# RWKV inputs: the receptance and the output gate's blended input computed for the 512 latent tokens alone

## What is computed

```python
def rwkv_prepare(h, mu, w_rkv, ...):
    xx = centred_shift(h) - h
    xr, xw, xk, xv, xa, xg = h[None] + xx[None] * mu[:, None, None, :]
    r, k, v = jnp.einsum('sbtd,sde->sbte', jnp.stack([xr, xk, xv]), w_rkv)
    ...                                   # decay from xw, a from xa
    g = jax.nn.sigmoid(xg @ g1) @ g2
    ...
    yc_f, yc_b, st_f, st_b = bidir(cxt, s0, s0, need_ctx)     # need_ctx is False in this layer
    yl_f, yl_b, _, _ = bidir(lat, st_f, st_b, True)
    out_l = readout(lat, yl_f, yl_b)
```

## Time and profile before

| quantity | value |
|---|---|
| median of three runs | 3681.42 us (3680.19 to 3684.13) |
| span of the profiled execution | 3676.6 us |
| its mean granted TensorE clock | 0.963 of full speed |
| TensorE busy | 3407.3 us (93%) |
| VectorE busy | 1631.8 us (44%) |
| ScalarE busy | 1158.3 us (32%) |
| GpSimd busy | 400.1 us (11%) |
| share of TensorE in the chain that ended last | 82% |

### The profile page before, as it was taken

One profiled execution on the slowest core, in us unless ns is written; L12 is line 12 of the kernel. 1 busy time (PEld: TensorE's weight loads), 2 busy tenths in 40 slices (PEclk: granted clock), 3 DMA queues, 4 the chain that ended last, 5 costly groups with the idle time before them and its releaser, 6 DMA issues.

```text
span 3676.6 us, 79518 instructions
## 1 busy us (share of the span) xinstructions
PE 3407.3 (93%) x35550; PEld 2653.0 (72%) x35550; DVE 1631.8 (44%) x3121; ACT 1158.3 (32%) x2449; POOL 400.1 (11%) x616
## 2 busy tenths in 40 slices
PE   7998998999999699899999997999989898899998
PEld 5767977788888488799999985688868776534333
DVE  3354455423323632467767773443444474312112
ACT  3342233312212333355555442322243332100001
POOL 0000122100000100222333320000011200100000
PEclk9999999999999899999999997899999999799999
DMA  5493153111111110000000002122211122589996
GB/s 192 149 351 107 49 242 115 69 69 69 69 47 69 65 46 24 9 6 6 5 6 5 6 4 100 69 92 92 92 67 47 61 92 107 242 372 414 413 428 292
DMA packets 35237, 437.41 MB, mean 119 GB/s; under 512 B 5025, under 2 KB 5633, under 8 KB 9169
## 3 DMA queue, kind: packets, MB, share of 16 engines
q1 hardware_dynamic: 29664, 413.44, 28.1%
q0 software_dynamic: 5232, 18.89, 1.6%
HBM read 425.49 MB, written 6.82 MB: 118 GB/s over the span
## 4 chain that ended last, share of the span: by engine, by line
PE 82%; DMA 7%; DVE 6%; ACT 4%; issue 1%; POOL 0%; SPq 0%; DVEq 0%; ACTq 0%; POOLq 0%
PE ps L755 23%; PE ps L2050 8%; PE ps L2051 8%; PE ps L2052 8%; PE ps L2468 7%; PE ps L3825 6%; DMA part<-in_wu 4%; PE ps L2461 3%; PE ps L2475 2%; PE ps L1010 1%; PE ps L2583 1%; PE ps L2574 1%; PE ps L1327 1%; PE ps L3705 1%; PE ps L2304 1%
## 5 line engine op out<-in xcount | busy, mean ns | idle before, releaser
L755 PE MATMUL ps<-part 128*128 128x256 f32 (+1 forms) x4848 | 876.3, 343 | 43.1 <-DVE part L995 16.9
L755 PEld LDWEIGHTS ps<-part 128*128 128x128 f32 x4848 | 754.9, 193 | 161.3 <-issue 19.1
L2050 PE MATMUL ps<-part 128*128 128x512 f32 (+1 forms) x1536 | 549.8, 358 | 18.1 <-DVE part L2097 11.4
L2051 PE MATMUL ps<-part 128*128 128x512 f32 (+1 forms) x1536 | 549.0, 357 | 0.0
L2052 PE MATMUL ps<-part 128*128 128x512 f32 (+1 forms) x1536 | 548.8, 357 | 0.0
L3825 PE MATMUL ps<-part 128*64 128x512 f32 x1536 | 375.5, 609 | 26.0 <-DMA part<-in_wg 10.3
L2074 DVE TENSOR_TENSOR part<-part 128x1024 fp32r<-128x1024 f32 x128 | 158.4, 1237 | 494.0 <-ACT part L2063 494.0
L2468 PE MATMUL ps<-part 64*64 64x64 f32 x9984 | 341.6, 219 | 11.0 <-DVE part L2619 4.6
L2468 PEld LDWEIGHTS ps<-part 64*64 64x64 f32 x9984 | 316.1, 135 | 32.8 <-DVE part L2721 7.2
L2050 PEld LDWEIGHTS ps<-part 128*128 128x128 f32 x1536 | 290.4, 189 | 67.5 <-DVE part L2097 12.6
L2051 PEld LDWEIGHTS ps<-part 128*128 128x128 f32 x1536 | 290.6, 189 | 46.0
(11 more groups left out here) (418 smaller groups left out, 4339.0 us busy)
## 6 DMA issues: line engine op xcount, KB each, us to landing
part<-in_ada_w SPq DMA_DIRECT2D x36, 2048.0 KB, 9.6
part<-in_mlp_w SPq DMA_DIRECT2D x32, 2048.0 KB, 7.5
part<-in_wg SPq DMA_DIRECT2D x32, 2048.0 KB, 14.5
part<-in_wu SPq DMA_DIRECT2D x32, 2048.0 KB, 12.8
part<-in_wd SPq DMA_DIRECT2D x32, 2048.0 KB, 13.8
part<-in_b_in SPq DMA_DIRECT2D x8, 2048.0 KB, 7.6
part<-in_ab_w_in SPq DMA_DIRECT2D x7, 2048.0 KB, 8.3
part<-in_rkv SPq DMA_DIRECT2D x6, 2048.0 KB, 7.4
```

The costliest lines, as they stand in the source:

```text
L755: mm = pe.e.matmul(ps[:, j * n:j * n + n], lhs, rhs, start=k == ks[0] and i == 0, stop=k == ks[-1] and i == 2)
L2050: pe.e.matmul(ps, wh[:, k, :], hi[:, k, x0:x1], start=k == 0, stop=False)
L2051: pe.e.matmul(ps, wh[:, k, :], lo[:, k, x0:x1], start=False, stop=False)
```

## The change

The function `rw_tokens` gives the latent range alone for "r" and both ranges otherwise. With it, for r: the blend has 512 columns instead of 770, the rounding and the rest are made for one range, the products go over `LAT`, and the copies from PSUM too. For g the blend has 512 columns instead of 770; its hidden product is as it was. v, k, w and a are untouched.

```diff
+def rw_tokens(what):
+    return TOKENS[:1] if what == "r" else TOKENS
...
-    def blend(out, i, k, what):
-        v.e.scalar_tensor_tensor(out=out, in0=a.xx[:, k, 1:771], scalar=a.mu[:, i * 8 + k:i * 8 + k + 1],
-                                 in1=a.hp[:, k, 1:771], op0=MUL, op1=ADD).then_inc(*v.up(("rw blend", what, k)))
+    def blend(out, i, k, what, end=771):
+        v.e.scalar_tensor_tensor(out=out, in0=a.xx[:, k, 1:end], scalar=a.mu[:, i * 8 + k:i * 8 + k + 1],
+                                 in1=a.hp[:, k, 1:end], op0=MUL, op1=ADD).then_inc(*v.up(("rw blend", what, k)))
...
-        for x0, x1, o in TOKENS:
+        for x0, x1, o in rw_tokens(what):
             v.e.tensor_tensor(dst[:, k, x0:x1], src[:, k, x0:x1], a.hi[:, k, o:o + x1 - x0], SUB).then_inc(
...
-    for i, what, before in ((4, "a", "w"), (5, "g", "a")):
+    for i, what, before, end in ((4, "a", "w", 771), (5, "g", "a", 513)):
         for k in range(8):
             v.wait_ge(K.at("rw hidden", before, k))
-            blend(a.mix[:, k, 1:771], i, k, what)
+            blend(a.mix[:, k, 1:end], i, k, what, end)
...
-            blend(a.mix[:, k, 1:771], 0, k, "r")
+            blend(a.mix[:, k, 1:513], 0, k, "r", 513)
...
-        through(w.columns(g, "rw " + what, 2 * (g % 4), x, BOTH, ready, wide=g % 4 == 0))
+        through(w.columns(g, "rw " + what, 2 * (g % 4), x, LAT if what == "r" else BOTH, ready, wide=g % 4 == 0))
...
-        for x0, x1, o in TOKENS:
+        for x0, x1, o in rw_tokens(what):
             s.e.activation(a.hi[:, k, o:o + x1 - x0], src[:, k, x0:x1], ACT.Copy).then_inc(*s.up(("rw hi", what, k)))
...
-    def columns(g, n, dst):
+    def columns(g, n, dst, parts=BOTH):
...
-            for pi, (x0, x1) in enumerate(BOTH):
+            for pi, (x0, x1) in enumerate(parts):
...
-        columns(g, "rw r", a.rT)
+        columns(g, "rw r", a.rT, LAT)
...
-    columns(3, "rw r", a.rT)
+    columns(3, "rw r", a.rT, LAT)
```

## The result

| kernel | median, us | range | ratio to before (95% interval) |
|---|---|---|---|
| before | 3682.78 | 3680.19 to 3688.09 (4 runs) | |
| changed | 3659.9 | 3657.93 to 3664.6 (4 runs) | 0.9936 (0.992 to 0.9951) |

The medians differ by 22.9 us, 0.62%. The forecast was 22.7 us less and 3658.7 us. On another chip the changed kernel took 3660.36 us against 3683.73 us, ratio 0.9933 (0.9921 to 0.9946).

A forecast was written before the change was run, and what follows sets the result against it. TensorE's matmul stream was taken to bound r; 22.7 us cut there, with no wait added and the other engines' savings off the path, gave 3681.42 - 22.7 = 3658.7 us, range 3653 to 3664.

The forecast's parts named there:

- TensorE's stream: In r, bound by TensorE's matmuls alone: 192 matmuls of 256 columns go, taking 22.7 us off the end.
- No fixed part per matmul: In r's products, 512- and 256-column matmuls (234 and 119 ns) were said to cost the same per column.
- The rival that a removed matmul gives back less: In r, taking a 256-column matmul out frees only some 98 ns: gain 18.8 us, time 3662.6; chance 0.04.
- Ahead of r: In g's hidden product and before: lighter blends and roundings lie off the path, gain nothing; r still starts at 1289.96.
- Three things that had to keep up: In r, now 45.2 us: r's own input, the weights' split and the weight panels still fit, no wait added.
- the split's margin: In r: copy, rounding and rest of a weight group take 4.5 us against 11.2 us, some 6.7 us to spare.
- that rival: In r, a wait replaces the gain: a 12.5 us split chain costs about 4 us, time 3662.7; chance 0.03.
- The panels of weights: In r, the next panel is issued at 1312.4 and first rounded 43 us later; 15 us would do, no wait.
- The pause and what is behind: After r, the 3.29 us pause before v stays, and everything later moves forward unchanged.
- The 0.4 us that two copies less might bring: In v's wide group, ScalarE has two copies of r's last group instead of four: up to 0.4 us, counted as none.
- The whole rest, 2315 us, moves forward as one piece: From v on, each engine's program is unchanged and loads are issued on releases, so 2315 us shift together.
- The clock: After TensorE's pauses, spells at 1.2 GHz cost 1.3 to 1.7 us; two more or fewer give 3662.1 or 3655.3, within 0.87.

The follow-up runs named there:

- Products alone: Kernel before with only r's products and their bank copies cut to the latents, blends, roundings and rests unchanged: 3657.8 us, ratio 0.9926.
- blends alone: Kernel before with only the blends of g and r cut to 512 columns: 3681.85 us against 3682.04, ratio 0.9995.

## Why the prediction was right

**TensorE's stream: right.** 22.7 us were forecast and 22.86 measured inside the stage. Products alone give all of it, blends alone none. That the medians differ by 22.9 us too is partly luck: the interval of the ratio allows 18 to 29 us, and single executions scatter by several us. The spacing of the 512-column matmuls when they stand alone, 5.60 us for 24, was forecast at 5.62.

**"No fixed part per matmul": wrong, and it did no harm for this size.** That step read 234 and 119 ns as proof that a matmul costs its columns and nothing else. The sizes below 256 show a floor of 108 to 110 ns, which goes with the weight columns, and 256 columns stand just above it. Two sizes can't show a floor that lies below both. That 256 columns do was luck for this step. The price was still right, since it was read from 24 short matmuls in a row, floor and all. With a 128-token context the same reasoning by columns would have forecast 11.4 us and been 8 x (2.63 - 1.42) = 9.7 us off. The rival that a removed matmul gives back less, 98 ns, was wrong for 256 columns, and so was the range's 18.8 us, which rests on it alone; its thought, that the stream has a floor, was right, and its size was not.

**Ahead of r: right** in that nothing there got shorter or longer: 44.25 us from the first hidden product to r, in every profile. "The start of r stays at 1289.96" was wrong as an absolute time, 1298.83. VectorE's saving was put at 7.8 us and is 8.0; ScalarE's at 5.5 and is 4.3; neither shows in the time.

**Three things that had to keep up: right**, and the split's margin, worked out at 6.7 us and some 6.2 by the trace, bears 5.8 us more and not 11.7. What that step left out is the order on VectorE behind it: had the split been late, its price would not have been a small excess per group but v's whole chain pushed back. My 4 us for that rival had no such term.

**The panels of weights: right.** The next panel is issued at 1321.54, 22.7 us after r's start (22.5 worked out), and nothing waits for it.

**The pause and what is behind: right in size**, 3.30 us as before. The 0.4 us that two copies less might bring in v's wide group did not come (69.45 against 69.43). The scan's first VectorE instruction is at 1488.78; counted from r's start that is 189.95 us, against 1501.41 - 1289.96 = 211.45 in before, 21.5 less: 22.85 gained, 1.33 lost to k's spell. "The whole rest, 2315 us, moves forward as one piece" holds within the scatter: from v's first matmul on it is 2311.7 and 2315.1 us in the two profiles of the changed kernel. The 4.8 us kept between span and median is mostly scatter as well; in one and the same execution of the changed kernel time and span are 1.8 us apart (3660.71 and 3658.9). The absolute 1478.7 of the forecast was a bad landmark, as the start of r moves by up to 9.7 us between executions.

**The clock: right in price for most spells, small in effect.** A spell was put at 1.3 to 1.7 us. Of the 22 seen behind these two pauses 18 cost 1.2 to 1.4 us and four, all behind the pause before v, 2.1 to 2.6. "k's pause of 2.18 us was followed by none" was read from one profile and isn't the rule. In the profiled execution after the change one was added there, which the range allowed for.

## What to carry to other kernels

In a TensorE-bound stage, price a removed matmul by the release times of whoever empties its banks, on rows of the very shape that goes, and not by columns. For the fp32r matmuls here, each with a load of 128 weight columns, the floor takes over below some 240 moving columns (an estimate, 110 ns at 0.457 ns a column); trimming columns there brings next to nothing (110 to 108 ns from 128 to 64), and cutting each piece of r into two cost 10 us. A shorter stage is also a shorter cover, so list what hides in it with its margin, and see what stands behind each of these on its engine. A region that a change no longer writes is room, and a pause of one chain can be paid from it by a buffer for the first piece alone.

## What the runs showed of the hardware that I had not expected

A stream of fp32r matmuls, each with its own load of 128 weight columns, doesn't go below 108 to 110 ns per matmul, with 128 or 64 moving columns; with 64 weight columns it went down to 60 ns at 128 moving columns.

A pause of TensorE of 3.3 us or more was followed by a spell at 1.2 GHz in 12 of 12 cases and one of 2.18 us in 10 of 14, each spell costing 1.2 us or more on top of the pause. So making v's first piece early brought 3.8 us inside the stage where the pause itself became 2.2 us shorter.
